# A two-block transformer on one core: four of the eight query projections of a sparse attention moved behind its keys and values

## What is computed

```python
proj = h @ w_in
q, c, q_idx, k_idx, w_idx = jnp.split(proj, [s1, s2, s3, s4], axis=-1)
c = rmsnorm(c, g_kv)                                   # latent, 256 wide
s_idx = jnp.einsum('bqhd,bsd->bqhs', qib, k_idx) * IDX_DIM ** -0.5
score = jnp.einsum('bqhs,bqh->bqs', jax.nn.relu(s_idx), wb)
score = jnp.where(admissible[None], score, -jnp.inf)
top_val, top_idx = lax.top_k(score, n_sel)             # 64 keys of 272 for each query
q_lat = jnp.einsum('bqhd,hcd->bqhc', qb, w_uk)         # 8 heads of 128
logits = jnp.einsum('bqhc,bqkc->bhqk', q_lat, c_sel) * ATT_HEAD_DIM ** -0.5 + bias
p = jax.nn.softmax(logits, axis=-1)
u = jnp.einsum('bhqk,bqkc->bqhc', p, c_sel)
out = jnp.einsum('bqhc,hcd->bqhd', u, w_uv) @ w_out
```

## Time and profile before

| | |
|---|---|
| median of 3 runs | 1282.58 us (1282.28 to 1283.68) |
| the profiled execution's own time | 1282.58 us |
| its span, first to last instruction | 1280.8 us |
| TensorE busy | 1238.3 us (97%) |
| VectorE, ScalarE, GpSimd busy | 837.7 (65%), 678.5 (53%), 102.9 (8%) |
| mean granted TensorE clock | 0.969 of full speed |
| weight units loaded | 383 of 512 KB, median 3.5 us from issue to landing |

### The profile page before, as it was taken

How to read it: one execution, slowest core, us unless ns; L and a number is a source line. 1 busy time by engine, 2 the same in 40 slices (tenths; PEclk the granted TensorE clock), 3 DMA queues, 4 the chain that set the end, 5 groups by cost and what they waited for, 6 DMA issues and landing times.

```text
span 1280.8 us, 26984 instructions
## 1 busy us (share of the span) xinstructions
PE 1238.3 (97%) x9812; PEld 1193.5 (93%) x9812; DVE 837.7 (65%) x1300; ACT 678.5 (53%) x1096; POOL 102.9 (8%) x116
## 2 busy tenths in 40 slices
PE   8999999999999899999999869999999998999999
PEld 8998999999998689999999769999999876999998
DVE  5677866665568547666668897666556566766543
ACT  5535655544445436665555856555445346665432
POOL 2000200000100211000021131000010013100000
PEclk9998999999999669999999989999999999999999
DMA  6432455556555015555664435556557421555663
GB/s 240 157 102 96 163 175 172 178 167 197 187 194 163 17 33 181 181 188 188 193 207 145 146 124 190 180 184 194 193 188 248 143 83 37 188 186 180 203 194 113
DMA packets 57484, 208.08 MB, mean 162 GB/s; under 512 B 6336, under 2 KB 7488, under 8 KB 57168
## 3 DMA queue, kind: packets, MB, share of 16 engines
q1 hardware_dynamic: 57136, 204.04, 49.3%
q0 software_dynamic: 288, 3.21, 0.6%
HBM read 206.18 MB, written 1.05 MB: 162 GB/s over the span
## 4 chain that ended last, share of the span: by engine, by line
PE 86%; DVE 8%; issue 3%; ACT 2%; POOL 1%; DVEq 0%; POOLq 0%; ACTq 0%
PE acc L849 27%; PE acc L851 26%; PE acc L850 26%; DVE w_lo L1273 2%; PE acc L1100 2%; PE pa L1074 1%; PE acc L949 1%; ACT pe L824 1%; POOL sqsum L406 1%; DVE t_s L1697 1%; DVE x_lo L1295 0%; DVE nmx L1829 0%; DVE score L1562 0%; PE stat L1090 0%; PE pa L936 0%
## 5 line engine op out<-in xcount | busy, mean ns | idle before, releaser
L849 PE MATMUL acc<-x_hi,w_hi 128*128 128x256 f32 (+1 forms) x1792 | 514.3, 287 | 6.5 <-DVE w_lo L1273 3.2
L1273 DVE TENSOR_TENSOR w_lo<-w_raw,w_hi 128x1024 fp32r<-128x1024 f32 x383 | 469.0, 1227 | 74.3 <-ACT w_hi L473 73.4
L851 PE MATMUL acc<-x_hi,w_lo 128*128 128x256 f32 (+1 forms) x1792 | 510.4, 285 | 0.0
L850 PE MATMUL acc<-x_lo,w_hi 128*128 128x256 f32 (+1 forms) x1792 | 509.9, 285 | 0.0
L473 ACT CAST w_hi<-w_raw 128x1024 fp32r<-128x1024 f32 x383 | 398.5, 1045 | 186.2 <-PE acc L851 182.8
L849 PEld LDWEIGHTS acc<-x_hi,w_hi 128*128 128x128 f32 x1792 | 340.3, 190 | 13.4 <-issue 6.3
L851 PEld LDWEIGHTS acc<-x_hi,w_lo 128*128 128x128 f32 x1792 | 340.5, 190 | 0.0
L850 PEld LDWEIGHTS acc<-x_lo,w_hi 128*128 128x128 f32 x1792 | 339.2, 189 | 0.3
L851 PE MATMUL acc<-m_hi,w_lo 128*128 128x256 f32 x512 | 141.3, 276 | 0.0
L849 PE MATMUL acc<-m_hi,w_hi 128*128 128x256 f32 x512 | 141.3, 276 | 0.0
L850 PE MATMUL acc<-m_lo,w_hi 128*128 128x256 f32 x512 | 141.3, 276 | 0.0
(11 more groups left out here) (302 smaller groups left out, 1610.4 us busy)
## 6 DMA issues: line engine op xcount, KB each, us to landing
w_raw<-weights SPq DMA_DIRECT2D x383, 512.0 KB, 3.5
bias<-bias_rows POOLq DMA_DIRECT2D x1, 2048.0 KB, 8.9
h<-hT SPq DMA_DIRECT2D x4, 272.0 KB, 5.3
bias<-bias_rows POOLq DMA_DIRECT2D x1, 1088.0 KB, 8.8
outT<-h SPq DMA_DIRECT2D x4, 256.0 KB, 4.7
con<-constants SPq DMA_DIRECT2D x1, 913.0 KB, 8.9
par<-cols SPq DMA_DIRECT2D x1, 84.0 KB, 2.0
a<-w_a SPq DMA_DIRECT2D x1, 32.0 KB, 9.1
```

Of the source, the lines that this page charges most:

```text
L849: nc.tensor.matmul(out, wh, xh[:, k, tok], start=first and n == 0, stop=False)
L850: nc.tensor.matmul(out, wh, xl[:, k, tok], start=False, stop=False)
L851: ins = nc.tensor.matmul(out, wl, xh[:, k, tok], start=False, stop=last and n == ntiles - 1)
L1273: V.tensor_tensor(w_lo[:, slot, :], w_raw[:, slot, :], w_hi[:, slot, :].bitcast(F32), ALU.subtract)\
```

## The change

The core of the diff, in the order of the program:

```diff
-          ("dsa_c", 4), ("dsa_qidx", 4), ("dsa_q", 8), ("uk", 2), ("uv", 2), ("dsa_out", 8),
+          ("dsa_c", 3), ("dsa_qidx", 4), ("dsa_q", 4), ("uk", 2), ("uv", 2), ("dsa_q2nd", 4), ("dsa_out", 8),
...
-        relu_s = get("relu_s", [P, 2, T])
+        relu_s = get("relu_s", [P, 4, T])
# ScalarE
+            act.wait_ge(s_("kidx_ready"), 1)
+            act.dma_start(kidx[IDX_DIM:2 * IDX_DIM, :], kidx[0:IDX_DIM, :]).then_inc(s_("kidx_doubled"), 16)
...
+            for i in range(8):
+                if i % 4 == 0:
+                    ahead("uk", i // 4)
+                if i % 4 < 3:
+                    act.wait_ge(s_("kh_psum"), 3 * (i // 4) + i % 4 + 1)
+                else:
+                    act.wait_ge(units_used, FIRST["uk"] + i // 4 + 1)
+                nc.scalar.copy(kh[:, i, :], acc[i % 4][:, 0:T]).then_inc(s_("kh_copied"), 1)
+                index_relu(8 + i)
...
+                    if t == 1:
+                        ahead("dsa_q2nd", 3)
                     nc.scalar.activation(pe1[:, t % 2, 0:n], lg1[:, t % 2, 0:n], ACT.Exp, bias=nmx1[:, t:t + 1],
# TensorE
+            for m in range(4):
+                project_query(m)
+                index_scores(2 * m)
+                index_scores(2 * m + 1)
             pe.wait_ge(s_("clo_ready"), 2)
+            for i in range(8):
...
+                for c in range(2):
+                    wh = w_hi[:, u % RING, (2 * j + c) * P:(2 * j + c + 1) * P]
+                    wl = w_lo[:, u % RING, (2 * j + c) * P:(2 * j + c + 1) * P]
+                    nc.tensor.matmul(acc[j][:, 0:T], wh, c_hi[:, c, :], start=(c == 0), stop=False)
+                    nc.tensor.matmul(acc[j][:, 0:T], wh, c_lo[:, c, :], start=False, stop=False)
+                    ins = nc.tensor.matmul(acc[j][:, 0:T], wl, c_hi[:, c, :], start=False, stop=(c == 1))
...
+                index_scores(8 + i)
...
-            pe.wait_ge(acc_free, MT["uv"])
+            project_query(4)
+            project_query(5)
             scores1(0)
+            project_query(6)
             for t in range(2 * ATT_HEADS + 2):
+                if t == 1:
+                    project_query(7)
                 if t + 1 < 2 * ATT_HEADS:
                     scores1(t + 1)
# VectorE
+            for m in range(4):
+                project_query(m)
+                if m == 0:
+                    trail_latent()
+                add_index_score(2 * m)
+                add_index_score(2 * m + 1)
+            for i in range(8):
+                take_top(0, [i])
+                add_index_score(8 + i)
+                if i % 4 == 0:
+                    ahead("uk", i // 4)
             take_top(1, [0, 1])
             ahead("uv", 0)
             take_top(1, [2, 3, 4])
             ahead("uv", 1)
             take_top(1, [5, 6, 7])
+            project_query(4)
+            project_query(5)
...
+                if t == 0:
+                    project_query(6)
                 if t:
                     dve.wait_ge(s_("ri1_ready"), k + 1)
...
+                if t == 1:
+                    project_query(7)
```

More of the change, by code:

```diff
@@ L618, in _ @@
             root("mix1", allt)
-            for k in range(1, 4):
+            for k in range(1, 3):
                 ahead("dsa_c", k)
@@ new lines, in _ @@
+            for g in range(6):
+                k, b = g // 3, g % 3
+                if b == 0:
+                    ahead("uv", k)
+                n = min(P, T - b * P)
+                if b < 2:
+                    act.wait_ge(s_("vh_psum"), 2 * k + b + 1)
+                else:
+                    act.wait_ge(units_used, FIRST["uv"] + k + 1)
+                nc.scalar.copy(vh[0:n, b, k * 512:(k + 1) * 512], acc[g % 4][0:n, :]).then_inc(s_("vh_copied"), 1)
+            for m in range(3):
+                ahead("dsa_q2nd", m)
@@ L1004, in _ @@
             gated_mlp(0, allt)
-            four("dsa_c", 0, MT["dsa_c"], 0, 0, x_hi, x_lo, allt, (x_ready, 8 * XN["mix1"]), norm=("mix1", allt))
+            for j in range(3):
+                u = FIRST["dsa_c"] + j
+                pe.wait_ge(acc_free, MT["dsa_c"] + j - 3)
+                unit(u, u % RING, acc[j][:, 0:T], x_hi, x_lo, allt, True, True,
+                     gate=(x_ready, 8 * XN["mix1"]) if j == 0 else None)
+                if j == 0:
+                    sum_squares("mix1", allt)
             for n in range(2):
@@ L1048, in _ @@
[L1048 to L1064 removed]
+                if j == 0:
+                    pe.wait_ge(lo_ready, u + 1)
@@ new lines, in _ @@
+                if j < 3:
+                    ins.then_inc(s_("kh_psum"), 1)
+                else:
+                    ins.then_inc(units_used, 1)
+                index_scores(8 + i)
+            for g in range(6):
+                k, b = g // 3, g % 3
+                u = FIRST["uv"] + k
+                if b == 0:
+                    pe.wait_ge(lo_ready, u + 1)
+                keys = slice(b * P, min((b + 1) * P, T))
+                out = acc[g % 4][0:keys.stop - keys.start, :]
+                if g < 4:
+                    pe.wait_ge(s_("kh_copied"), g + 5)
+                else:
+                    pe.wait_ge(s_("vh_copied"), g - 3)
+                for c in range(2):
+                    wh = w_hi[:, u % RING, 4 * c * P:4 * (c + 1) * P]
+                    wl = w_lo[:, u % RING, 4 * c * P:4 * (c + 1) * P]
+                    nc.tensor.matmul(out, c_hi[:, c, keys], wh, start=(c == 0), stop=False)
+                    nc.tensor.matmul(out, c_lo[:, c, keys], wh, start=False, stop=False)
+                    ins = nc.tensor.matmul(out, c_hi[:, c, keys], wl, start=False, stop=(c == 1))
+                if b < 2:
+                    ins.then_inc(s_("vh_psum"), 1)
+                else:
+                    ins.then_inc(units_used, 1)
@@ L1506, in _ @@
             inverse("mix1", allt)
-            for k in range(4):
+            for k in range(3):
                 unit_done("dsa_c", k)
```

172 lines of the change are left out of this document (72 added, 100 removed).

## The result

| | us |
|---|---|
| changed kernel, median of 4 runs (1259.41, 1260.60, 1260.71, 1283.19) | 1260.65 |
| kernel before, median of 4 runs (1282.28 to 1283.68) | 1282.91 |
| ratio, without the run at 1283.19 | 0.9827, 95% interval 0.9812 to 0.9841 |
| profiled execution after: time, span, mean granted clock | 1259.41, 1257.6, 0.988 |

The forecast was 1260.5 us.

A forecast was written before the change was run, and what follows sets the result against it. It took VectorE's top-k as the bound before the first values, then TensorE at half clock through attention 1. From 1282.58 us, -2.8 - 17.7 - 1.6 = -22.1 us gave 1260.5 us, range 1255.5 to 1280.5.

The forecast's parts named there:

- One unit of `dsa_c` less: Before the first values: one `dsa_c` unit fewer on TensorE, -3.0 us; its load and splits worth nothing.
- Copies bank by bank: At keys and values: copying bank by bank removes a 0.7 us stall behind the copies, twice, -1.4 us.
- Single index scores: Second block: a single score takes as long as a pair, so eight singles for four pairs cost +3.3 us.
- TensorE is the bound at the head: Head of attention 1: TensorE, not VectorE, is the bound; one stall of 1.4 us replaces two of 1.6.
- First values: Start of attention 1's first values: at 421.6 us instead of 424.43, -2.8 us.
- The clock holds: Attention 1: TensorE's clock stays up behind the one stall, giving 1260.5 us; chance 0.50.
- the second rival: The clock falls inside attention 1, or in some runs only: about half the gain, some 1270 us; chance 0.05.
- The first rival: The clock falls all the same, attention 1 at 5.78 us a head: 1278.6 us; chance 0.37.
- Attention at 3.4 us a head: Attention 1 at full clock: 7.5 heads take 25.5 us instead of 43.2, -17.7 us.
- `dsa_out` at full clock: Start of `dsa_out`: its 3.5 us at half clock would run at full clock, -1.6 us.
- The sum: Whole kernel: -2.8 - 17.7 - 1.6 = -22.1 us, forecast 1260.5 us, by its own bounds 1256 to 1264.
- Index scores lock the engines: Around the keys: scores couple TensorE and VectorE, 7.2 us longer with the clock fallen, 1285.8 us; chance 0.04.

The follow-up runs named there:

- e5: Kernel before with only the first part of the change (three `dsa_c` units, keys doubled by a transfer): 1281.57 us, ratio 0.9994.
- e6: Changed kernel with the second block's index scores in pairs behind keys 1, 3, 5 and 7 instead of single: 1281.88 us.
- e11: e6 with four and seven unread matmuls filling its two waits ahead of the transposes: 1260.41 us, ratio 0.9825.
- e1: Kernel before with six unread matmuls in each of its two waits at the head of attention 1: 1266.14 us, ratio 0.9863.
- e3: Changed kernel with all four moved query units ahead of score 0, none between scores: 1264.25, 1264.47, 1284.57 and 1287.59 us.
- e4: Changed kernel with five unread matmuls in its wait at the head of attention 1 and four before `dsa_out`: 1259.88 us.
- e12: e10 with the split for query unit 7 two rounds earlier, and unread matmuls before step 1's transposes and before `dsa_out`: 1255.56 us.
- e10: e6 with the splits behind query units 5, 6 and 7 moved later into attention 1, as in e9: 1258.59 us, ratio 0.9815.
- e2: Kernel before with the twelve fillers of e1 as transposes instead of matmuls: 1268.41, 1265.13, 1266.26 and once 1288.13 us.
- e7: Changed kernel with the weight split behind query unit 7 moved later into attention 1: 1259.17 us, ratio 0.9812.
- e8: The changed kernel itself, unchanged, run five more times to count runs in which the clock falls in attention 1: 1260.83 us.
- e9: Changed kernel with the splits behind query units 5, 6 and 7 moved later into attention 1: 1263.17 us, ratio 0.9850.

## Why the prediction was right

The time was right within 0.2 us, and that close it was by luck: one term was mis-sized by 0.8 us, one of 1.6 us didn't come, and stages that the change doesn't touch gave 2.4 us. What was right is the mechanism, two waits becoming one, with the clock staying up behind it, and the size of the largest term.

- **One unit of `dsa_c` less, -3.0.** e5 has it alone: -3.3 to the first values. Right. The doubling transfer landed 3.3 us after its issue at 357.2 us, 12 us ahead of the first index score. Hidden, as said.
- **Copies bank by bank, -1.4.** Not tried alone. The timeline of before has a wait of 0.57 us at the keys and one like it at the values, that of the changed kernel has neither. Single scores and keys stand 1.60 us apart in the changed kernel, 0.755 for the matmuls and 0.84 for the score, with no wait between; that is the pitch of the sum. The terms up to here and the next one add up: with two moved units behind it score 0 was to come at 411.4 us, 6.8 us sooner than in the kernel before, and behind the mark it comes 6.8 us sooner.
- **Single index scores, +3.3.** Right on TensorE (0.72 against 0.73 us, e6: 3.4 us). But as a cost it is mostly hidden: without it VectorE sets the pace, and the first values come only 0.8 us sooner (e11). What I called the risk of the sum, "the stall grows by as much, and the clock is at more risk", is what e6 shows, in ten runs of ten, though by a saving of TensorE's work and not by cheaper single scores.
- **TensorE is the bound at the head, one stall of 1.4 us.** Right: one wait, released by the probabilities of step 1, of 1.67 us. Mask at 407.5 us, inside the bound of 411.4.
- **First values, -2.8.** Mis-sized: -3.6. The stall was longer than the 1.4 us by 0.3, but from the end of unit 7 to the first values are 3.13 us where the sum has 3.1. The term that failed is "scores 0 and 1 (1.4, each between units, priced as the pairs of index scores)": scores 0, 1 and 2 stand 3.04 and 3.27 us apart, a unit takes 2.85, so the two cost 0.6 us together. Here scores of 128 rows cost less between units (0.2 and 0.4 us) than those of 64 rows (0.75).
- **The clock holds, 0.50; falls, 0.37.** The mechanism and the size are shown by e1: 17 us from matmuls that compute nothing. That it isn't certain was right as well: it holds in eight runs of nine. The falls in some runs only, for which the second rival had 0.05, are what one of the four runs of the result shows, though at the upper level and not half-way. The reason given for the clock's staying up, one stall and not two, is not the whole of it: with two waits of 1.16 and 1.10 us (e3) it stayed up in two runs of four. The first rival's price was off, for it gave 1278.6 and the one high run took 1283.2; attention 1 alone accounts for 17.3 us of the 22 or so that lie between it and the others. That run has no trace; its mean clock leaves room for some 12 us more at half clock elsewhere (60 less 48, an estimate).
- **Attention at 3.4 us a head, -17.7.** 25.98 us against 43.24: -17.3. Logits of one head and the next stand 3.42 us apart.
- **`dsa_out` at full clock, -1.6.** Wrong: the clock fell at about 445.3 us, in the wait of 1.20 us behind the last values, and `dsa_out` ran at 0.50 for 3.3 us, about as long as before (3.5). I had reasoned only about whether the fall at 423 us comes, not about what the end of attention 1 does once the clock is up. e3, e4, e11 and e12 have `dsa_out` at 1.00, so the term is there to be had, by luck or by fillers. Its size was about right: e4 and e11, which later on have the clock at half for 14 us, as the changed kernel has, take 810.1 and 810.5 us from `dsa_out` to the end where the changed kernel takes 812.2.
- **The sum.** -3.6 - 17.3 = -20.8 us in the stretch (with rounding) against -20.5 by the terms without `dsa_out`. The missing 1.6 is made up by -1.45 before the mark and -0.9 behind it, which belong to no step of the sum.
- **Index scores lock the engines (slower, 0.04).** It didn't come; TensorE never waits among the keys.

## What to carry to other kernels

When TensorE waits twice in a row after a dense stretch, price the wait by what the clock does behind it: here 3 us of waiting cost 17. A cheap test comes before any reordering: fill the wait with matmuls that nobody reads, and see which part of the time was clock. Time such a kernel several times, for the same program can stand on two levels. And look at who is second before taking work from TensorE: where that is VectorE, the work saved becomes a wait, and at such a place it can cost far more than it saved (e6: -3.4 us of work, +21 us of time) until VectorE is relieved too (e10).

## What the runs showed of the hardware

- TensorE's clock followed the same instructions in two ways: the changed kernel, e2 and e3 have runs on two levels 17 us or more apart, with nothing between, and the higher ones have the lower mean clock (0.962 to 0.965 against 0.980 to 0.988). How many runs of each kernel fell stands beside its waits in the table of the experiments.
- Two matmuls that use 64 rows each took 0.73 us as a pair and 0.72 us as one alone.
- A transpose of 128x128 took one pass of the two that a matmul of 128x128 in the same type takes (0.82 against 1.50 us for six). Twelve of them in two waits went with full clock in three runs of four, where without them it was at half in all.
- Where the clock fell near the start of `dsa_out`, it did so at another place in every kernel's trace. Worked out from the granted clock in windows of 0.5 us, it fell 0.5 us ahead of `dsa_out`'s first matmul in e7 and 0.1 us in the changed kernel, and behind it by 0.3 us in e10, 0.5 in e8, 0.6 in e1, 0.9 in e9 and 1.0 in e2. So with e2 and e9 it fell in dense matmuls, behind the thin work: work at half clock is not always the work that brought the clock down.
- One hand-over between engines was as long at either clock: `dsa_out` waits 1.20 us for VectorE's split of the last head at half clock and at full clock (447.77 us in e11).
